# Two transformer blocks on one core: how rotations, score masks, sinks and gates are made, and where four pieces of work stand

## The chip, the cores and the metric

The kernel runs on one core of one Trainium2 chip. The metric is the device time of one execution in microseconds (us); of several runs, the median. PE is TensorE, ACT ScalarE, DVE VectorE, POOL GpSimd, and SP the engine that issues the loads.

## What is computed

Input is x, 512 tokens by 1024 features, float32. `first_block` runs twice (two layers: latent attention with 8 heads and a depthwise convolution of 31 taps beside it, output projection, gated feed-forward part with a short convolution), then `second_block` once. The parts that the change touches, cut from the reference:

```python
def rope(x, pos):                       # second block: queries and keys, heads of 64
    x1, x2 = xf[..., :half], xf[..., half:]
    return concatenate([x1 * cos - x2 * sin, x2 * cos + x1 * sin])
...
ckv = vmap(compress)(stack([k_c, v_c]), cmp_pos, cmp_w1, cmp_w2)     # gelu(blocks @ w1) @ w2, 31 blocks
o_cmp, p_cmp = compressed_attention(qn, ckv[0], ckv[1], t)
o_slc = selected_attention(qn, k_s, v_s, idx, t)
o_win = banded_attention(qn, k_w, v_w, NSA_WINDOW, None)
gates = sigmoid(g_n).reshape(B, S, NSA_KV, NSA_GROUP, NSA_BRANCHES)
o_nsa = gates[..., 0:1] * o_cmp + gates[..., 1:2] * o_slc + gates[..., 2:3] * o_win
o_swa = banded_attention(qw, kw, v_sw, SWA_WINDOW, sinks)            # window 128, a sink per head
    # s masked outside the band; m = max(s, sk); den = sum(exp(s - m)) + exp(sk - m)
```

With 512 tokens every block is selected, so `o_slc` is plain causal attention. In `first_block` the softmax runs over all 512 keys.

## The kernel before

Activations lie transposed, 128 features by 512 tokens per chunk. Every large product is exact to float32 by halves: weights come from memory into `raw` (a ring of four slabs), ACT rounds a slab into `w_hi` (`split`, L1083), DVE subtracts for `w_lo` (L1445), and PE does three matmuls per chunk (`mm3`, L516 to L518). `w_hi` and `w_lo` hold two slabs, so slab n+2 can be split only when PE has finished slab n. Each engine runs its own list of instructions in the order written; semaphores connect them (`wait_ge`, `then_inc`; a helper `Tally` only counts). No scheduler reorders anything: what stands earlier in an engine's list holds up what stands behind it.

**Attention of a layer of `first_block`** (PE L662, L691, L703). Work goes in 16 units, a pair of heads by 128 queries. In step s PE does `scores(s)`, `turn(s - 2)` (transposes of the probabilities) and `values(s - 3)`. DVE's `attend` takes the negative maximum (L1638) and the reciprocal of the sums (L1630), with four convolution taps (L1578) between units; 124 taps in all have to be done by the end. ACT's `attend` does the exponentials (L1227), `normalise` (L1209: scaling by the reciprocal, a pair of heads at a time) and `turned` (L1216: transposes out of PSUM). After units 0 to 2 ACT and DVE each split one slab, S_UKV + 1 + SPL, which is slab S_O + 1, a part of the output projection's weights.

**Projections of `second_block`** (`T_ORDER`, 13 slabs: `vc`, and then 12 chunks that are rotated, `ROPED`: kc, ks, kw, kx, four qn, four qx). PE puts slab i into bank i % 4. ACT copies the bank into `tz` (L1313). The rotation needs the two halves of 32 features of each head exchanged: PE multiplies `tz` by a permutation matrix (`swap_halves`, L776, float32, two passes) into bank 4 or 5, and DVE's `rope` (L1742, L1743, L1752) forms cos times `tz` plus sin times the swapped bank. DVE's loop also does, per i, a split, one of eight scalings of x (L1775, i = 3 to 10) and at i = 2 and 3 `blocks` (L1723 to L1729: the overlapping key and value blocks for `compress`), at i = 4 and 5 `blocks_low` (L1734). Then four slabs of untransposed values and gate columns (`VG`, 408 columns) go into banks 0 to 3, and PE computes `compress` (8 slabs, matmuls of 256 columns). ACT copies the values (L1332, L1333), forms the gates by Sigmoid (L1335) and the Gelu (L1340), and loads the table of log and exp (L1088) before it copies `hid`, `kcT` and `vcn` (L1345 to L1349), on which the small products L844, L849 and then L863 wait. The exponentials of the compressed scores come at L1352.

**Attention of `second_block`**: 48 units in the same three-stage scheme (`scores2`, `turn2`, `values2`). A unit sees n key chunks of 128 (1 to 4; in the sliding-window units, 16 of the 48, one at t = 0 and two otherwise). Its scores go to bank pair `S2_B[u % 2]`; on top PE adds masks as bf16 matmuls (diagonal L892, previous chunk L891) and, in sliding-window units, writes the sink into the column behind the scores (L895, float32, one column), for each head of the pair.

## Time and profile before

| | |
|---|---|
| median of 3 runs | 1944.41 us (1942.99 to 1944.85) |
| the profiled execution's own time | 1946.59 us |
| its span | 1944.8 us |
| PE, DVE, ACT busy | 96%, 68%, 48% of the span |
| mean granted PE clock | 0.985 |
| first layer, second layer, second block, last projection part | roughly 0 to 600, 600 to 1225, 1225 to 1530, 1530 to 1945 us |

All times of views are microseconds from the span's start. A clock of 1.00 is 2.4 GHz, 0.50 is 1.2 GHz. A timeline row gives start, duration, engine, line, operation, tiles, count of merged instructions, and in brackets how long the engine had been idle before and what ended that. A matmul's duration includes its drain; the pace of a stream is the distance of its starts.

### The profile page before, as it was taken

The numbers are of one execution on the slowest core, as the hardware profiler recorded it, in microseconds if no ns is written. First come the engines' busy times: TensorE is split into PE (matmuls) and PEld (weight loads), VectorE is DVE, ScalarE is ACT, GpSimd is POOL, SyncE is SP. The second block draws the span as 40 slices with busy tenths as digits, with TensorE's granted clock in tenths as the row PEclk, the third lists the DMA queues.
The fourth block names the chain that finished last, engine by engine and source line by source line (L and its number), as shares of the span: only waits on it lengthen the run. The fifth ranks groups of instructions, "written<-read, shape, count | busy, mean of one in ns | idle before, by whom it ended". The sixth has DMA issues, their size and how long they took to land.

```text
span 1944.8 us, 27183 instructions
## 1 busy us (share of the span) xinstructions
PE 1875.1 (96%) x9099; PEld 1477.2 (76%) x9099; DVE 1322.9 (68%) x1890; ACT 927.3 (48%) x1473; POOL 176.2 (9%) x130
## 2 busy tenths in 40 slices
PE   6999999999999999999999999998898999999998
PEld 5775688888888775678888888777565778888887
DVE  6899667777655799767777655773767377777544
ACT  5468554444433457664444433324656554444322
POOL 0000220000132000130000033000012300000010
PEclk9999999999999999999999999998899999999999
DMA  5220133333234321023333233334000223333332
GB/s 164 69 78 23 33 97 95 97 94 93 84 99 110 79 79 34 12 87 98 97 97 97 79 97 104 88 82 130 1 1 1 76 65 97 97 97 88 89 96 74
DMA packets 285096, 154.47 MB, mean 79 GB/s; under 512 B 16949, under 2 KB 283095, under 8 KB 285015
## 3 DMA queue, kind: packets, MB, share of 16 engines
q1 hardware_dynamic: 284596, 153.26, 27.4%
q8 instruction: 46, 0.75, 0.2%
q14 instruction: 35, 0.29, 0.0%
q10 hardware_dynamic: 419, 0.17, 0.0%
HBM read 151.31 MB, written 2.10 MB: 79 GB/s over the span
## 4 chain that ended last, share of the span: by engine, by line
PE 83%; DVE 8%; issue 4%; ACT 4%; DMA 0%; DVEq 0%; SPq 0%; ACTq 0%
PE bank L516 24%; PE bank L518 24%; PE bank L517 24%; DVE cacc L1578 2%; PE bank L887 1%; PE bank L929 1%; PE bank L908 1%; DVE w_lo L1445 1%; DVE nmax L1638 1%; PE bank L662 1%; ACT w_hi L1083 1%; PE bank L895 1%; PE bank L530 0%; ACT pr L1209 0%; DMA x_in<-in_x 0%
## 5 line engine op out<-in xcount | busy, mean ns | idle before, releaser
L1083 ACT ACTIVATE w_hi<-raw 128x1024 fp32r<-128x1024 f32 (+3 forms) x345 | 336.9, 984 | 605.2 <-PE bank L518 599.2
L1445 DVE TENSOR_TENSOR w_lo<-raw,w_hi 128x1024 fp32r<-128x1024 f32 (+3 forms) x345 | 407.4, 1188 | 314.6 <-ACT w_hi L1083 313.1
L516 PE MATMUL bank<-h_hi,w_hi 128*128 128x512 f32 x1448 | 575.9, 398 | 5.9 <-DVE w_lo L1445 5.6
L518 PE MATMUL bank<-h_hi,w_lo 128*128 128x512 f32 x1448 | 564.8, 390 | 0.0
L517 PE MATMUL bank<-h_lo,w_hi 128*128 128x512 f32 x1448 | 564.7, 390 | 0.0
L516 PEld LDWEIGHTS bank<-h_hi,w_hi 128*128 128x128 f32 x1448 | 272.5, 188 | 71.6 <-issue 11.3
L517 PEld LDWEIGHTS bank<-h_lo,w_hi 128*128 128x128 f32 x1448 | 272.4, 188 | 61.6 <-issue 6.3
L518 PEld LDWEIGHTS bank<-h_hi,w_lo 128*128 128x128 f32 x1448 | 272.4, 188 | 57.2
L516 PE MATMUL bank<-a_hi,w_hi 128*128 128x512 f32 x528 | 206.1, 390 | 0.0
L518 PE MATMUL bank<-a_hi,w_lo 128*128 128x512 f32 x528 | 205.5, 389 | 0.0
L517 PE MATMUL bank<-a_lo,w_hi 128*128 128x512 f32 x528 | 205.4, 389 | 0.0
L1578 DVE SCALAR_TENSOR_TENSOR cacc<-u_pad,lc,cacc 128x512 f32<-128x512 f32 x240 | 168.1, 751 | 1.6
L1526 DVE TENSOR_TENSOR zr<-bank,rstd 128x512 f32<-128x512 f32 x132 | 90.8, 688 | 83.1 <-PE bank L518 68.8
L1532 DVE SCALAR_TENSOR_TENSOR tz<-zr,lc,tz 128x511 f32<-128x511 f32 x176 | 131.9, 750 | 19.5 <-DVE tz L1532 6.8
L1149 ACT ACTIVATE a_hi<-tz 128x512 f32 (+1 forms) x66 | 41.7, 633 | 160.7 <-DVE tz L1540 160.7
L518 PEld LDWEIGHTS bank<-a_hi,w_lo 128*128 128x128 f32 x528 | 99.1, 188 | 20.7
L517 PEld LDWEIGHTS bank<-a_lo,w_hi 128*128 128x128 f32 x528 | 99.1, 188 | 20.5
L516 PEld LDWEIGHTS bank<-a_hi,w_hi 128*128 128x128 f32 x528 | 99.1, 188 | 20.3
L1542 DVE TENSOR_TENSOR a_lo<-tz,a_hi 128x512 f32 x66 | 45.7, 693 | 61.5 <-ACT a_hi L1149 61.5
L1145 ACT ACTIVATE tz<-zr,lc 128x512 f32<-128x512 f32 x88 | 71.1, 808 | 28.8 <-DVE zr L1526 28.8
L1931 POOL TENSOR_TENSOR sq<-x 128x512 f32 (+1 forms) x14 | 27.4, 1959 | 616.3 <-DVE x L1704 616.3
L1532 DVE SCALAR_TENSOR_TENSOR tz<-zr,cols,tz 128x510 f32<-128x510 f32 x88 | 65.9, 749 | 9.5 <-DVE tz L1532 1.7
(295 smaller groups left out, 2227.7 us busy)
## 6 DMA issues: line engine op xcount, KB each, us to landing
raw<-in_w_up SPq DMA_DIRECT2D x132, 512.0 KB, 3.8
raw<-in_w_in SPq DMA_DIRECT2D x39, 512.0 KB, 3.9
raw<-in_w_down SPq DMA_DIRECT2D x48, 384.0 KB, 3.3
raw<-in_w_down SPq DMA_DIRECT2D x48, 320.0 KB, 3.1
raw<-in_w_o SPq DMA_DIRECT2D x16, 512.0 KB, 3.4
raw<-in_cmp_w SPq DMA_DIRECT2D x8, 512.0 KB, 3.8
raw<-in_w_out SPq DMA_DIRECT2D x8, 512.0 KB, 3.7
raw<-in_w_uq SPq DMA_DIRECT2D x8, 288.0 KB, 2.9
```

The lines of the kernel that those rows point to most:

```text
L516: mm(o, wh, mh, start=start, stop=False)
L517: mm(o, wh, ml, start=False, stop=False)
L518: return mm(o, wl, mh, start=False, stop=stop)
L1083: last = A_(dst(w_hi), src(raw), ACT.Copy)
L1145: A_(tz[:, s, :], zr[:, s % 2, :], ACT.Identity, bias=c_b(ch), scale=c_w1(ch)).then_inc(z1_done.sem, 1)
L1149: A_(a_hi[:, bass.ds(i * 2 + j, 1), :], tz[:, 2 * j + 1:2 * j + 2, :], ACT.Copy).then_inc(ah_done.sem, 1)
L1445: last = v.tensor_tensor(dst(w_lo), src(raw), dst(w_hi).bitcast(f32), ALU.subtract)
L1526: v.tensor_tensor(zr[:, s % 2, :], bank[s][:, :], rstd[:, 0, :], ALU.mult).then_inc(zr_done.sem, 1)
L1532: ins = v.scalar_tensor_tensor(tz[:, s, a:b], zr[:, s % 2, a + sh:b + sh], tap(n, ch), tz[:, s, a:b], ALU.mult, ALU.add)
L1542: v.tensor_tensor(a_lo[:, bass.ds(i * 2 + j, 1), :], tz[:, 2 * j + 1:2 * j + 2, :], a_hi[:, bass.ds(i * 2 + j, 1), :].bitcast(f32), ALU.su ...
L1578: ins = v.scalar_tensor_tensor(cacc[:, c, :], src, wc, cacc[:, c, :], ALU.mult, ALU.add)
L1931: link(p.tensor_tensor(sq[:, :], chunk, chunk, ALU.mult))
```

## The change

1. **Halves swapped by ACT.** PE's `swap_halves` is gone. After the copy into `tz`, ACT copies the same bank four more times, 32 partitions each and into the neighbour's place, into a new tile `swapped`, which DVE's `rope` reads instead of a bank. PE's slab i waits until slab i - 4's swap is made. The values go to banks 4, 5, 1, 2.
2. **Blocks later.** `blocks` moves from i = 2, 3 to i = 6, 9, `blocks_low` with ACT's rounding of `xe` from i = 4, 5 to i = 8, 11, and the scalings of x from i = 3 to 10 to i = 5 to 12.
3. **Gates by exponential.** ACT computes exp(-g) (L1348 of the changed kernel), with the negated scale in a new tile `r_neg`; DVE adds 1 and takes the reciprocal. The load of the table of log and exp moves behind `vcn`.
4. **Sinks once per bank pair.** Only units with t < 2 write the sink, before their scores; units with t = 2 and 3 find it in the bank. A unit with one chunk puts it in columns 128 to 255, so that the sink's column is 256 in all. The two masks of a unit with two chunks become one matmul of 256 columns with `band_b`.
5. **Third pair scaled sooner.** In the first block's attention, ACT does `normalise(2)` and `turned(1)` right behind the exponentials of unit 2, and DVE `inverse(2)`; the split of slab S_O + 1 moves to the end (ACT behind step 17, DVE behind step 18).

```diff
-            def swap_halves(r):
-                pe.wait_ge(rc_done.sem, r + 2)
-                if r >= 2:
-                    pe.wait_ge(rope_done.sem, r - 1)
-                mm(bank[4 + r % 2][:, :], const[:, K_SWAP:K_SWAP + P], tz[:, r % 2, :], start=True, stop=True)\
-                    .then_inc(sw_done.sem, 1)
...
+                if i >= 5:
+                    pe.wait_ge(sw_done.sem, i - 4)
...
-                if i >= 2:
-                    swap_halves(i - 2)
...
-            swap_halves(len(ROPED) - 1)
+            pe.wait_ge(sw_done.sem, len(ROPED) - 2)
...
+                c0 = first_col(b, t)
+                if b == SC_SWA and t < 2:
+                    for e in range(2):
+                        mm(o[e][:, 2 * P:2 * P + 1], ones[0:1, :], sinks[0:1, 2 * c + e:2 * c + e + 1], start=True, stop=True)
...
                     if n == 2 and b == SC_SWA:
-                        mm(o[e][:, 0:P], eye_b[:, :], prev_b[:, :], start=False, stop=False)
-                    last = mm(o[e][:, (n - 1) * P:n * P], eye_b[:, :], diag_b[:, :], start=False, stop=True)
-                    if b == SC_SWA:
-                        last = mm(o[e][:, n * P:n * P + 1], ones[0:1, :], sinks[0:1, 2 * c + e:2 * c + e + 1], start=True, stop=True)
+                        last = mm(o[e][:, 0:2 * P], eye_b[:, :], band_b[:, :], start=False, stop=True)
+                    else:
+                        last = mm(o[e][:, c0 + (n - 1) * P:c0 + n * P], eye_b[:, :], band_b[:, P:2 * P], start=False, stop=True)
...
                 attend(2)
-                split(L, g, S_UKV + 1 + SPL)
+                normalise(2)
+                turned(1)
                 for s in range(3, SU + 4):
                     attend(s)
+                    if s == SU + 1:
+                        split(L, g, S_UKV + 1 + SPL)
...
+                for h in range(4 * (i > 0)):
+                    last = A_(swapped[h * 32:(h + 1) * 32, (i - 1) % 2, :], bank[i % 4][(h ^ 1) * 32:((h ^ 1) + 1) * 32, :], ACT.Copy, scale=sc)
+                if i > 0:
+                    last.then_inc(sw_done.sem, 1)
...
-                A_(gates[:, t * NG:(t + 1) * NG], bank[t][:, 2 * P:2 * P + NG], ACT.Sigmoid,
-                   scale=r_in[:, t:t + 1]).then_inc(gate_done.sem, 1)
+                A_(gates[:, t * NG:(t + 1) * NG], VG_B[t][:, 2 * P:2 * P + NG], ACT.Exp,
+                   scale=r_neg[:, t:t + 1]).then_inc(gate_exp.sem, 1)
...
-                link(v.tensor_tensor(tz[:, 3, :], bank[4 + r % 2][:, :], const[:, K_SIN:K_SIN + SEQ], ALU.mult))
+                link(v.tensor_tensor(tz[:, 3, :], swapped[:, r % 2, :], const[:, K_SIN:K_SIN + SEQ], ALU.mult))
...
-                if 3 <= i < 3 + KD:
-                    c = i - 3
+                if 5 <= i < 5 + KD:
+                    c = i - 5
...
+            dve.wait_ge(gate_exp.sem, NT)
+            link(v.tensor_scalar(gates[:, :], gates[:, :], 1.0, None, ALU.add))
+            v.reciprocal(gates[:, :], gates[:, :]).then_inc(gate_done.sem, 1)
```

Three places in the order of the instructions. First, ACT at the start of the first block's attention, from the copy of unit 0's transposes on (`pr` probabilities, `pt` their transposes, `w_hi` a split slab). Before:

```order
L1209 ACTIVATE pr<-pr,rinv 128x512 x2
L1216 ACTIVATE pt<-bank 128x512 x2
L1226 REGISTER_ALU
L1227 ACTIVATE pr,rsum<-bank,nmax 128x512
L1226 REGISTER_ALU
L1227 ACTIVATE pr,rsum<-bank,nmax 128x512
L1083 ACTIVATE w_hi<-raw 128x1024
L1226 REGISTER_ALU
L1227 ACTIVATE pr,rsum<-bank,nmax 128x512
L1226 REGISTER_ALU
L1227 ACTIVATE pr,rsum<-bank,nmax 128x512
L1206 REGISTER_ALU
```

and now:

```order
L1213 ACTIVATE pr<-pr,rinv 128x512 x2
L1220 ACTIVATE pt<-bank 128x512 x2
L1230 REGISTER_ALU
L1231 ACTIVATE pr,rsum<-bank,nmax 128x512
L1230 REGISTER_ALU
L1231 ACTIVATE pr,rsum<-bank,nmax 128x512
L1210 REGISTER_ALU
L1213 ACTIVATE pr<-pr,rinv 128x512 x2
L1220 ACTIVATE pt<-bank 128x512 x2
L1230 REGISTER_ALU
L1231 ACTIVATE pr,rsum<-bank,nmax 128x512
```

The scaling of unit 2 and the copy of unit 1's transposes now stand ahead of the exponentials of unit 3, and no split stands there.

Second, ACT from the gates to the compressed scores. Before:

```order
L1335 ACT_TABLE_LOAD
L1335 ACTIVATE gates<-bank,r_in 128x24 x4
L1083 ACTIVATE w_hi<-raw 128x1024 x4
L1340 ACT_TABLE_LOAD
L1340 ACTIVATE hidc<-bank 62x256
L1083 ACTIVATE w_hi<-raw 128x1024 x4
L1340 ACTIVATE hidc<-bank 62x256
L1088 ACT_TABLE_LOAD
L1345 ACTIVATE hid<-bank 128x62 x4
L1347 ACTIVATE kcT<-bank 128x62
L1349 ACTIVATE vcn<-bank 31x128
L1352 ACTIVATE cs<-cs 128x496 x2
```

and now:

```order
L1348 ACTIVATE gates<-bank,r_neg 128x24 x4
L1087 ACTIVATE w_hi<-raw 128x1024 x4
L1353 ACT_TABLE_LOAD
L1353 ACTIVATE hidc<-bank 62x256
L1087 ACTIVATE w_hi<-raw 128x1024 x4
L1353 ACTIVATE hidc<-bank 62x256
L1357 ACTIVATE hid<-bank 128x62 x4
L1359 ACTIVATE kcT<-bank 128x62
L1361 ACTIVATE vcn<-bank 31x128
L1092 ACT_TABLE_LOAD
L1365 ACTIVATE cs<-cs 128x496 x2
```

Of three table loads two are left, and the last stands behind `vcn`.

Third, PE in one sliding-window unit with t = 2 (L887 scores, L908 transposes, L929 values). Before:

```order
L887 MATMUL bank<-k_kx,qx 128x256 x2
L891 MATMUL bank<-prev_b,eye_b 128x128
L892 MATMUL bank<-diag_b,eye_b 128x128
L895 MATMUL bank<-sinks,ones 128x1
L891 MATMUL bank<-prev_b,eye_b 128x128
L892 MATMUL bank<-diag_b,eye_b 128x128
L895 MATMUL bank<-sinks,ones 128x1
L908 MATMUL bank<-const,pr_86 128x128 x2
```

and now, two such units and the beginning of the one that follows, which has t = 0:

```order
L893 MATMUL bank<-k_kx,qx 128x256 x2
L897 MATMUL bank<-band_b,eye_b 128x256 x2
L912 MATMUL bank<-const,pr_87 128x128 x2
L933 MATMUL bank<-pt_88,v_78 64x128 x4
L893 MATMUL bank<-k_kx,qx 128x256 x2
L897 MATMUL bank<-band_b,eye_b 128x256 x2
L912 MATMUL bank<-const,pr_87 128x128 x4
L933 MATMUL bank<-pt_88,v_78 64x128 x2
L891 MATMUL bank<-sinks,ones 128x1 x2
L893 MATMUL bank<-k_kx,qx 128x128 x2
L899 MATMUL bank<-band_b,eye_b 128x128 x2
```

Behind the scores stand two matmuls where six stood; the sinks are written only ahead of the scores of t = 0 and 1.

## Rows read from the trace of the kernel before

**Rows 1.** The page, part 1 (busy us, share) and PE's waits over the span (total, times, longest).

```profile
PE 1875.1 (96%) x9099; PEld 1477.2 (76%) x9099; DVE 1322.9 (68%) x1890; ACT 927.3 (48%) x1473; POOL 176.2 (9%) x130
...
PE bank L691 <- ACT pt L1216: 13.2, 10, 3.7
```

**Rows 2.** Timeline of PE, projections of the second block.

```profile
1234.21 0.39 PE L516 MATMUL bank<-h_hi,w_hi 128*128 128x512 f32 x1
...
1239.65 1.02 PE L776 MATMUL bank<-tz,const 128*128 128x512 f32 x2
...
1246.00 1.02 PE L776 MATMUL bank<-tz,const 128*128 128x512 f32 x2
...
1307.41 1.12 PE L776 MATMUL bank<-tz,const 128*128 128x512 f32 x2 [0.85 <-ACT tz L1313]
1307.97 0.75 PE L516 MATMUL bank<-w_hi,h_hi 128*128 128x408 f32 x1
```

**Rows 3.** Timeline of ACT: a split and a copy there, two copies of 64 partitions earlier.

```profile
1293.10 1.06 ACT L1083 ACTIVATE w_hi<-raw 128x1024 fp32r<-128x1024 f32 x1 [4.80 <-PE bank L518]
...
133.54 1.22 ACT L1201 ACTIVATE kT<-bank 64x512 f32<-64x512 f32 x2 [0.51 <-PE bank L518]
```

**Rows 4.** Timeline of DVE in the projections' loop: `blocks`, iteration 5, and a query's last step.

```profile
1254.95 2.69 DVE L1723 COPY xe<-vc_raw 64x248 f32<-64x248 f32 x8
...
1259.00 1.22 DVE L1445 TENSOR_TENSOR w_lo<-raw,w_hi 128x1024 fp32r<-128x1024 f32 x1
...
1262.12 2.79 DVE L1752 TENSOR_TENSOR k_kw<-tz 64x512 f32<-64x512 f32 x4
...
1276.43 0.69 DVE L1752 TENSOR_TENSOR qn<-tz 128x512 f32<-128x512 f32 x1
```

**Rows 5.** Timelines of ACT and PE from the gates to the compressed scores.

```profile
1330.14 1.28 ACT L1335 ACT_TABLE_LOAD   x1
...
1334.48 0.39 PE L516 MATMUL bank<-w_hi,xe_hi 128*128 128x256 f32 x1 [3.84 <-DVE w_lo L1445]
...
1348.82 1.28 ACT L1088 ACT_TABLE_LOAD   x1
...
1350.60 1.08 PE L844 MATMUL bank<-hid,w2k 128*128 128x62 f32 x4 [1.41 <-ACT hid L1345]
...
1353.02 7.04 PE L863 MATMUL bank<-kcT,qn 64*128 64x31 f32 x64 [0.36 <-ACT vcn L1349]
...
1363.44 1.20 ACT L1352 ACTIVATE cs<-cs 128x496 f32<-128x496 f32 x2 [10.47 <-DVE cs L1802]
```

**Rows 6.** Timeline of PE: masks and sinks of a sliding-window unit with two chunks.

```profile
1427.51 0.23 PE L891 MATMUL bank<-prev_b,eye_b 128*128 128x128 bf16 x1
1427.57 0.22 PE L892 MATMUL bank<-diag_b,eye_b 128*128 128x128 bf16 x1
1427.72 0.38 PE L895 MATMUL bank<-sinks,ones 1*128 1x1 f32 x2
...
1428.56 0.44 PE L908 MATMUL bank<-const,pr 128*128 128x128 f32 x2
```

**Rows 7.** First layer's attention: timelines of DVE and PE.

```profile
151.01 1.23 DVE L1445 TENSOR_TENSOR w_lo<-raw,w_hi 128x1024 fp32r<-128x1024 f32 x1 [1.45 <-ACT w_hi L1083]
152.15 1.28 DVE L1638 TENSOR_REDUCE nmax<-bank 128x1 f32<-128x512 f32 x2
...
161.86 0.69 DVE L1638 TENSOR_REDUCE nmax<-bank 128x1 f32<-128x512 f32 x1 [1.90 <-PE bank L662]
...
156.08 1.97 PE L691 MATMUL bank<-const,pr 128*128 128x128 f32 x8 [3.74 <-ACT pt L1216]
```

**Rows 8.** Stretches: us, busy PE, PEld, DVE, ACT, POOL, granted clock, DMA.

```profile
156.00:160.00 4.00, 3.92 (x25) 3.26 (x25) 3.93 (x8) 3.74 (x10) 0.00 (x0) 0.50 0.23 78
...
1421.48:1432.15 10.67, 10.67 (x90) 7.32 (x88) 6.35 (x22) 5.70 (x22) 1.58 (x2) 1.00 0.00 0
1353.00:1357.00 4.00, 3.98 (x38) 3.98 (x38) 0.00 (x0) 0.00 (x0) 0.00 (x0) 0.50 0.07 24
```

More of the change, by code:

```diff
@@ L107, in keys_of, with first_col @@
     return (max(0, t - 1), min(2, t + 1)) if b == SC_SWA else (0, t + 1)
+def first_col(b, t):
+    return P if b == SC_SWA and t == 0 else 0
 HALVES = [0]
@@ L174, in build @@
         lneb = sb("lneb", [P, 1])
+        r_neg = sb("r_neg", [P, NT])
         lc = sb("lc", [P, LCOLS])
@@ L238, in build @@
         v2 = at("v2", [P, NT, 3 * P], 32 * KB)
+        swapped = at("swapped", [P, 2, SEQ], 68 * KB)
         ct_all = at("ct_all", [P, PAIRS, NT, 2, P], 38 * KB)
@@ L260, in build @@
         STAT = bank[7]
+        VG_B = bank[4], bank[5], bank[1], bank[2]
         C_B, CT_B = (bank[4], bank[5]), (bank[6], bank[7])
@@ L809, in _ @@
                         k = i * VG_K + kk
-                        last = mm3(bank[t][:, 0:VG], (h_hi[:, k, tok], h_lo[:, k, tok]),
+                        last = mm3(VG_B[t][:, 0:VG], (h_hi[:, k, tok], h_lo[:, k, tok]),
                                    (w[0][:, kk, :], w[1][:, kk, :]), k == 0, k == KD - 1)
@@ L1311, in _ @@
                     act.wait_ge(rope_done.sem, i - 2)
+                sc = HD2 ** -0.5 if kind[0] == "q" else 1.0
                 dst = vc_raw[:, :] if kind == "vc" else tz[:, (i - 1) % 2, :]
-                A_(dst, bank[i % 4][:, :], ACT.Copy, scale=HD2 ** -0.5 if kind[0] == "q" else 1.0).then_inc(rc_done.sem, 1)
+                A_(dst, bank[i % 4][:, :], ACT.Copy, scale=sc).then_inc(rc_done.sem, 1)
+                for h in range(4 * (i > 0)):
+                    last = A_(swapped[h * 32:(h + 1) * 32, (i - 1) % 2, :], bank[i % 4][(h ^ 1) * 32:((h ^ 1) + 1) * 32, :], ACT.Copy, scale=sc)
+                if i > 0:
+                    last.then_inc(sw_done.sem, 1)
                 if i == 0:
@@ L1322, in _ @@
                     A_(r_in[:, :], bank[6][:, 0:NT], ACT.Copy).then_inc(rcol_done.sem, 1)
-                if i in (4, 5):
-                    t = i - 4
+                    A_(r_neg[:, :], bank[6][:, 0:NT], ACT.Copy, scale=-1.0).then_inc(rcol_done.sem, 1)
+                if i in (8, 11):
+                    t = i // 11
                     act.wait_ge(xe_f.sem, t + 1)
@@ L1328, in _ @@
                 step2(S2_V + i)
-            act.wait_ge(rcol_done.sem, 1)
+            act.wait_ge(rcol_done.sem, 2)
             for t in range(NT):
                 r = r_in[:, t:t + 1]
-                A_(v2[:, t, 0:2 * P], bank[t][:, 0:2 * P], ACT.Copy, scale=r).then_inc(v2_done.sem, 1)
-                A_(v2[:, t, 2 * P:3 * P], bank[t][:, 2 * P + NG:VG], ACT.Copy, scale=r).then_inc(v2_done.sem, 1)
+                A_(v2[:, t, 0:2 * P], VG_B[t][:, 0:2 * P], ACT.Copy, scale=r).then_inc(v2_done.sem, 1)
+                A_(v2[:, t, 2 * P:3 * P], VG_B[t][:, 2 * P + NG:VG], ACT.Copy, scale=r).then_inc(v2_done.sem, 1)
             for t in range(NT):
-                A_(gates[:, t * NG:(t + 1) * NG], bank[t][:, 2 * P:2 * P + NG], ACT.Sigmoid,
-                   scale=r_in[:, t:t + 1]).then_inc(gate_done.sem, 1)
+                A_(gates[:, t * NG:(t + 1) * NG], VG_B[t][:, 2 * P:2 * P + NG], ACT.Exp,
+                   scale=r_neg[:, t:t + 1]).then_inc(gate_exp.sem, 1)
             for t in range(2):
@@ L1362, in _ @@
                         st = 2 * (s % 4) + e
-                        A_(pr2[:, s % 3, e, 0:n], S2_B[s % 2][e][:, 0:n], ACT.Exp, bias=nmax[:, st:st + 1],
+                        c0 = first_col(b, t)
+                        A_(pr2[:, s % 3, e, 0:n], S2_B[s % 2][e][:, c0:c0 + n], ACT.Exp, bias=nmax[:, st:st + 1],
                            accum_out=rsum[:, st:st + 1]).then_inc(e_done.sem, 1)
@@ L1654, in _ @@
                 conv(3)
-                split(g, S_UKV + 1 + SPL)
+                inverse(2)
                 for s in range(3, SU + 5):
                     attend(s)
+                    if s == SU + 2:
+                        split(g, S_UKV + 1 + SPL)
                     conv(4)
@@ L1778, in _ @@
                     rope(i - 2)
-                if i == 2:
+                if i == 6:
                     blocks(0)
-                if i == 3:
+                if i == 9:
                     blocks(1)
-                if i in (4, 5):
-                    blocks_low(i - 4)
+                if i in (8, 11):
+                    blocks_low(i // 11)
             rope(len(ROPED) - 1)
```

25 lines of the change are left out of this document (12 added, 13 removed).

## The prediction, made before the changed kernel ran

> **What bounds the kernel now.** I read the page's part 1 first, then PE's waits, then the stretches, then the timelines of the four places that the change touches. PE is busy 96% of the span [rows 1], so outside a few places only matmul time that goes away shortens anything, and inside them a wait of PE does. Of what PE waits for, the largest is L691, transposes in the first block's attention: 13.2 us in 10 waits, at most 3.7 at a time [rows 1]. Behind such a wait the granted clock can stand at 0.50 [rows 8], so a wait costs more than its length. I take as unit of account the profiled execution (1946.59 us, span 1944.8); the median of the runs is 2.2 us lower, and I subtract the same gain from it. About 0.2%, 3.9 us, is what a measurement of this kernel can tell from no change.
>
> **Rotations.** A slab of projections takes PE 5.44 us (slab 2: 1234.21 to 1239.65), and with a swap the distance to the next swap is 6.35 [rows 2]: a swap costs 0.91 us, and there are 12, so 10.9. The last swap waits 0.85 for the last copy [rows 2], which goes too, since the values no longer need the last bank. That is 11.8 us of PE, plus some small waits for `w_lo` now.
>
> What takes their place is on ACT and DVE, which must fit into 5.44 us instead of 6.35. ACT: a split takes 1.06 and ACT is then idle for 4.80 before the next [rows 3]. A copy of 32 partitions by 512 from a bank is not in the trace; nearest is the copy of 64 partitions, two in 1.22, 0.61 each [rows 3]. Step i becomes 0.96 for the split, 0.6 for the copy, 4 x 0.61: 4.0 us, below 5.44. Bounds: a copy's time goes by its 512 columns, so I see no reason for less than 0.48 (its duration less an overlap) nor, since the split of 1024 columns takes 1.06, for more than that. DVE: iteration 5, with a key, runs from 1259.00 to 1264.91, 5.9 us (split, scaling of x, two products, four additions), a query's one addition takes 0.69 instead of 2.79 [rows 4], so 3.8; `blocks` takes 1254.95 to 1259.00, 4.05 [rows 4], `blocks_low` 1.2 by its size. The split for slab i+2 is ready in time if DVE has finished iteration i-1 some 4.2 us after the end of slab i. I carried this on slab by slab (slab end, ACT's split 0.26 later, DVE's split behind it or behind its last iteration). For the kernel before it gives the values' end 0.2 us from the traced one. For the changed kernel DVE lags 7 us behind a slab's end through the keys (iterations 3 to 5), 9 to 10 after iterations 6 and 9, which carry `blocks`, and PE waits 0.5 at slab 12 and 0.7 at the third slab of values, behind DVE's last rotations. So 12 less small waits: **12.0 us** (10.5 if each copy costs 1.0; 12.3 at 0.49). The scalings of x end two iterations later, and SP waits for them before it loads `compress`'s weights: that load would start near 1301.5 instead of 1301.9 and is wanted near 1309.7, covered. `r_neg` is one tiny copy more on ACT, in its idle time.
>
> **Gates and table loads.** ACT loads the Sigmoid's table for 1.28 us between the copies of the values and the third split of `compress`, for whose result PE waits 3.84 [rows 5]. Exp is in the table that is loaded anyway, so the wait becomes 2.56: 1.28 less. The second load, 1348.82 to 1350.10, stands ahead of `hid`; L844 waits 1.41 for that [rows 5]. Moved behind `vcn` it falls into ACT's 10.47 us of idle time before L1352 [rows 5]; L844 can start when the second L830 has ended, 1.2 us sooner. DVE's addition and reciprocal of 128x96 fall before the end of L863, where DVE waits for 10 us, and cost nothing; were that cover gone, 0.5. Sum **2.5 us**, at least 1.3 if one of the two is hidden by a split that is late anyway.
> The trace has the load at 1.28 us. The Trainium skill (ScalarE: Activation LUTs, What ACT_TABLE_LOAD costs) prices a switch at about 2.7 us with its drain; by that the two would be worth 5.3. The row decides.
>
> **Sinks and masks.** Behind the scores of a unit with two chunks come 1.05 us (1427.51 to 1428.56) of masks and sinks [rows 6]. A mask of 128 columns sets the pace at 0.06 (1427.51 to 1427.57), so two of 256 columns take 0.13 each at most, 0.25. With t = 2 and 3, 8 units, that is all: 0.8 less each, 6.4 us. With t = 0 and 1, also 8 units, the sinks stay: the two passes of one head go 0.38 [rows 6] with their drain, 0.31 by the start of what follows, so 0.6 for both heads. That leaves 0.2 less each, 1.6 to 1.8. Together **8.2 us** if PE stays the bound there. A unit then takes PE 1.8 to 2.1 us instead of 2.6; in a stretch of four units, 10.67 us, DVE is busy 6.35 and ACT 5.70 [rows 8], 1.6 and 1.4 us a unit, so there is just room. Bounds: 4 (DVE's evictions come through as waits), 9.
>
> **Third pair.** ACT's split stands behind the exponentials of unit 2, and DVE, after 1.45 of idle time, does its part from 151.01, so that the maximum of unit 3 starts at 152.15 and its exponentials behind that; unit 2 is scaled only behind them, and PE waits 3.74 for its transposes' turn [rows 7]; then the clock is at 0.50 from 156 to 160 [rows 8], scores come late and DVE idles 1.90 [rows 7]. With the new order the sums of unit 2 are there at 150.0 (where the split began), its scaling ends at 151.5, the copies of unit 1 at 152.4, about when PE has finished the scores of unit 4 (152.2): no wait of note. DVE's maximum of unit 3 starts at 150.15, 2.0 sooner, and unit 4's 2.0 sooner as well; behind it DVE sets the pace (3.9 us a unit: 1.28 for the maxima [rows 7], the rest taps) and the idle 2.07 does not come back: 4.1 us. PE meets one wait of 1.3 us at unit 3, whose scaling now stands behind the exponentials of unit 4; DVE's pace hides it. What is late next: at the end DVE must still do the split (1.2), between its last tap, some 5 us before PE wants the sums of the convolution, and those sums; it is covered, since slab S_O + 1 is wanted only after them. The loads that wait for this slab (S_O + 4, S_O + 5) start near 210 and are wanted near 228. So 4.1 per layer, **8.2 us** for two; at least 1.0 each (DVE's own idle time of 1.45 [rows 7], less 0.45 that it will wait for the sums), at most 5.
>
> **Sum.** 12.0 + 2.5 + 8.2 + 8.2 = 30.9: 1946.6 becomes 1915.7, the median 1944.4 becomes **1913.5 us**.
>
> **Rivals.**
> *A. The clock stays up in `compress`.* L863's 64 matmuls take 7.04 us [rows 5] at a granted 0.50 [rows 8], after waits of 3.84, 1.23 and 1.41. With the first at 2.56 and the third near 0.2 the clock might not fall: L863 would take 3.5 and the products before it 0.6 less, 4 us more gained: 1909.5. Against it: 2.3 us of `w_lo` waits stay in between, and the 1.23. 15%. What the page says goes the same way (the Trainium skill, TensorE: Matmul & The Clock Gate, HAM oscillation: idle gaps of PE throttle it, and the transition is paid again each time).
> *B. Part of the gain turns into new waits.* In the sliding-window units DVE or ACT becomes the bound (gain 4 instead of 8.2), or the first block's attention gives only the 1.0 per layer that DVE's idle time holds (2 instead of 8.2). For it: DVE works at its limit from 163 us on. 1918 to 1920. 17%.
> *C. Slower: the swap overloads ACT.* ACT becomes the pace of the projections when four copies and the rest pass 5.44, that is when a copy of 32 partitions costs over 0.97 us. To eat the gains elsewhere (18.9) and be 0.2% slower it must cost some 1.8: step 8.8, 12 steps, 40 us more than 5.44 each, less 11.8: 1944.4 - 18.9 + 28.5 = 1954. Nothing in the rows has 512 columns on ACT above 0.72. 2%.
> *D. It comes out level*, by B and C in part: 1%.
>
> **Numbers.** The forecast has 65% and its own range is 1910.5 to 1917. The range to hold 8 in 10 reaches into A and B: 1909 to 1920. Faster 0.97, same 0.01, slower 0.02.
>
> **What would show it.** No matmul of the swap between slabs, distances of 5.44 between slabs, `swapped` copies near 0.6 and the first matmul of the values some 12 us nearer to the projections' start; a wait near 2.6 in place of 3.84 and none for `hid`; no table load at the gates; 2.0 us between the starts of sliding-window units with t = 2 and 3; L691's waits down by 3.7 in each layer with the clock at 1.00 around 156 us, and the layer's end 4 us earlier. I am wrong if copies of 32 partitions take over 1 us, if PE waits over 2 us in all for `w_lo` in the projections, if DVE's maxima rather than PE set the pace of the sliding-window units, or if the 4 us of an attention come back as a wait before L735.

## The result, and the profile after

| | before | changed |
|---|---|---|
| median (range, runs) | 1944.19 us (1942.99 to 1944.85, 4) | 1922.26 us (1919.63 to 1924.50, 4) |
| profiled execution: own time, span | 1946.59, 1944.8 | 1924.50, 1922.4 |

The ratio is 0.989, 95% interval 0.9877 to 0.9902. The change gains 21.9 us where 30.9 were forecast; 1922.3 lies above the range of 1909 to 1920. Of all executions reported in this document one, of e1 below, took 2125.76 us at a mean granted clock of 0.841 against 0.979 to 0.995 elsewhere, and is left out of its ratio. The page of the changed kernel, part 1, and PE's waits over the span (total, times, longest):

```profile
PE 1856.1 (97%) x9019; PEld 1465.5 (76%) x9019; DVE 1322.8 (69%) x1892; ACT 955.2 (50%) x1521; POOL 176.0 (9%) x130
...
PE bank L700 <- ACT pt L1220: 9.2, 10, 1.7
PE bank L912 <- DVE pr L1886: 7.7, 7, 2.2
```

Against [rows 1] PE is busy 19.0 us less; its waits for the first block's transposes (L700 now) fell from 13.2 to 9.2, and a group has grown, the transposes of the second block that wait for DVE's scaling (L912), 7.7 us where the kernel before has 4.8.

Where the time went is read from seven markers on PE's timeline, each the start of the first or last row of merged matmuls with a given pair of operands: the first scores of a layer's attention and the sum over its convolution; the first matmul of `compress`; the first scores of the second block's attention (ks); the first and last of the sliding-window scores (kx); the last kw scores. The differences, in us:

| stage | before | changed | gain | forecast |
|---|---|---|---|---|
| first layer's attention | 82.58 | 79.55 | 3.0 | 4.1 |
| second layer's attention | 82.65 | 79.54 | 3.1 | 4.1 |
| sum of layer 2 to `compress` (projections, values) | 511.50 | 500.17 | 11.3 | 12.0 |
| `compress` to first ks scores | 33.58 | 29.35 | 4.2 | 2.5 |
| first ks to first kx scores | 48.24 | 48.26 | 0 | 0 |
| first to last kx scores | 42.75 | 40.53 | 2.2 | 8.2 |
| last kx to last kw scores | 44.73 | 47.89 | -3.2 | 0 |

One profile of each kernel stands behind this table, and a stage that two kernels share can differ between their profiles by where the clock fell: over the kernels below that leave a stage as it was, an attention takes 81.39 to 82.65 us, `compress` 32.25 to 33.58 and the kx stage 42.75 to 44.22.

**Projections.** ACT's timeline over one slab, and PE's row where the first values begin:

```profile
1233.47 1.06 ACT L1087 ACTIVATE w_hi<-raw 128x1024 fp32r<-128x1024 f32 x1
1234.55 0.60 ACT L1321 ACTIVATE tz<-bank 128x512 f32<-128x512 f32 x1
1235.18 2.39 ACT L1323 ACTIVATE swapped<-bank 32x512 f32<-32x512 f32 x4
1238.91 1.06 ACT L1087 ACTIVATE w_hi<-raw 128x1024 fp32r<-128x1024 f32 x1 [1.34 <-PE bank L527]
...
1289.63 0.34 PE L525 MATMUL bank<-w_hi,h_hi 128*128 128x408 f32 x1
```

Two splits are 5.44 us apart, as forecast; a copy of 32 partitions takes 0.60 (2.39 for four), and ACT still has 1.34 of idle time. The first values stand at 1289.63 instead of 1307.97 [rows 2]: 18.3 us sooner, of which 6.6 had been gained by the end of layer 2's attention, so 11.8 here, as forecast. PE's waits for `w_lo` in this stage are 0.51 (1284.04) and 0.59 (1299.33), against 0.5 and 0.7 in the forecast.

**Compress.** Timelines of PE and ACT:

```profile
1315.30 0.48 PE L525 MATMUL bank<-w_hi,xe_hi 128*128 128x256 f32 x1 [2.55 <-DVE w_lo L1459]
...
1331.65 6.29 PE L865 MATMUL bank<-kcT,qn 64*128 64x31 f32 x64 [0.36 <-ACT vcn L1361]
1331.62 1.28 ACT L1092 ACT_TABLE_LOAD   x1
1341.24 1.20 ACT L1365 ACTIVATE cs<-cs 128x496 f32<-128x496 f32 x2 [8.35 <-DVE cs L1818]
```

Against [rows 5]: the wait of 3.84 is 2.55, the one for `hid` is gone (0.36 for `vcn` is left ahead of L865), and the last table load lies inside ACT's idle time.

**Sliding-window units.** DVE, POOL and PE around the first eviction of `yw` (DVE's copy of a finished bank into the tile `yw`), then stretches (us, busy PE, PEld, DVE, ACT, POOL, granted clock, DMA):

```profile
1403.74 0.68 DVE L1849 COPY yw<-bank 128x512 f32<-128x512 f32 x1
1404.34 0.75 DVE L1870 TENSOR_REDUCE nmax<-bank 128x1 f32<-128x257 f32 x2
1404.50 1.04 POOL L1950 TENSOR_TENSOR sq<-yw 128x512 f32<-128x512 f32 x1 [181.79 <-DVE yw L1849]
1405.19 1.84 DVE L1886 TENSOR_SCALAR pr<-pr,rinv 128x256 f32<-128x256 f32 x2
1405.62 1.27 POOL L1951 TENSOR_TENSOR ssq<-ssq,sq 128x512 f32<-128x512 f32 x1
1407.09 0.67 PE L912 MATMUL bank<-const,pr 128*128 128x128 f32 x4 [0.94 <-DVE pr L1886]
...
1406.00:1410.00 4.00, 3.06 (x20) 2.39 (x20) 2.12 (x6) 1.65 (x6) 0.88 (x1) 0.70 0.00 0
1410.00:1414.00 4.00, 4.00 (x22) 2.41 (x20) 1.31 (x5) 1.51 (x5) 0.00 (x0) 0.50 0.00 0
```

The two scalings of 128x256, 0.62 us elsewhere in this stretch, take 1.84 while POOL squares and adds: they end at 1407.03, 0.14 behind the end of POOL's addition (1406.89). With the eviction and the maximum in front of them DVE needs 0.68 + 0.75 + 0.16 + 1.84 = 3.4 us for this unit; four units take PE 8.24 now (1396.67 to 1404.91), and the scores of t = 3 start 1.8 us behind those of t = 2 (1401.38, 1403.15; 2.0 forecast). So PE waits 0.94 (and again, 0.94 and 1.47, at the next two evictions), and the granted clock goes to 0.50 behind the wait. In the kernel before the clock was 1.00 there and PE had no such wait, although the same operation was slowed there as well. Its DVE and POOL, and the stretch of four units that follows the one of [rows 8]:

```profile
1423.34 0.62 DVE L1867 TENSOR_SCALAR pr<-pr,rinv 128x256 f32<-128x256 f32 x2
1431.84 1.46 DVE L1867 TENSOR_SCALAR pr<-pr,rinv 128x256 f32<-128x256 f32 x2
1431.61 1.27 POOL L1932 TENSOR_TENSOR ssq<-ssq,sq 128x512 f32<-128x512 f32 x1
...
1432.15:1442.82 10.67, 10.67 (x90) 7.32 (x88) 7.10 (x22) 5.64 (x22) 2.31 (x3) 1.00 0.01 2
```

The stretch of [rows 8], on which the forecast rests, ends 0.31 us into the slowed scaling, with DVE busy 6.35 us; this one has 7.10.

**First block's attention.** PE and DVE behind unit 3, then the stretches:

```profile
157.32 1.15 PE L700 MATMUL bank<-const,pr 128*128 128x128 f32 x8 [1.73 <-ACT pt L1220]
158.40 1.98 PE L712 MATMUL bank<-pt,vN 128*64 128x128 f32 x16
160.31 2.68 PE L671 MATMUL bank<-kT,qT 96*128 96x512 f32 x4
...
162.17 0.69 DVE L1652 TENSOR_REDUCE nmax<-bank 128x1 f32<-128x512 f32 x1 [0.95 <-PE bank L671]
...
156.00:160.00 4.00, 2.68 (x24) 2.41 (x24) 4.00 (x9) 3.81 (x10) 0.00 (x0) 0.79 0.00 0
160.00:164.00 4.00, 4.00 (x20) 2.18 (x18) 2.88 (x6) 2.61 (x6) 0.00 (x0) 0.78 0.00 0
```

The wait of 3.74 [rows 7] is gone and one of 1.73 has come at unit 3 (1.3 forecast); but the clock falls behind this one too, scores come late, and DVE idles 1.12 (0.95 and 0.17) of the 2.07 that it idled there before (1.90 in [rows 7] and 0.17).

### The profile page after: what moved, and what is told of

The parts are those of the page before. It is cut to its first block, busy times and chain, and to the rows that moved or that the text cites. A ratio compares the mean times of both kernels' runs of the same rounds, so it can differ in the third digit from the quotient of the medians.

```text
span 1922.4 us, 27065 instructions
## 1 busy us (share of the span) xinstructions
PE 1856.1 (97%) x9019; PEld 1465.5 (76%) x9019; DVE 1322.8 (69%) x1892; ACT 955.2 (50%) x1521; POOL 176.0 (9%) x130
## 4 chain that ended last, share of the span: by engine, by line
PE 82%; DVE 10%; ACT 4%; issue 4%; DMA 0%; DVEq 0%; SPq 0%; ACTq 0%
PE bank L525 24%; PE bank L527 24%; PE bank L526 24%; DVE cacc L1592 2%; PE bank L893 1%; PE bank L933 1%; DVE w_lo L1459 1%; PE bank L912 1%; DVE nmax L1652 1%; DVE pr L1886 1%; DVE nmax L1870 1%; PE bank L671 1%; PE bank L539 0%; ACT pr L1213 0%; DMA x_in<-in_x 0%
## 5 line engine op out<-in xcount | busy, mean ns | idle before, releaser
L525 PEld LDWEIGHTS bank<-h_hi,w_hi 128*128 128x128 f32 x1448 | 272.6, 188 | 68.3 <-issue 8.7
```

What stands on the lines that cost most here:

```text
L525: mm(o, wh, mh, start=start, stop=False)
```

## The experiments

Stage times of the profiled executions, by the same markers (att. 1 and 2: the two attentions; kx: first to last kx scores; kw: last kx to last kw scores):

| kernel | median us | att. 1 | att. 2 | compress | kx | kw |
|---|---|---|---|---|---|---|
| before | 1943.5 | 82.58 | 82.65 | 33.58 | 42.75 | 44.73 |
| e1 sinks, masks | 1941.23 | 81.39 | 81.61 | 32.63 | 38.97 | 46.37 |
| e2 third pair | 1938.43 | 78.25 | 79.59 | 32.40 | 42.76 | 46.13 |
| e3 rotations | 1933.95 | 81.47 | 81.63 | 33.37 | 44.22 | 44.73 |
| e4 gates, tables | 1942.28 | 82.21 | 82.46 | 27.50 | 44.22 | 46.01 |
| e5 changed, again | 1921.40 | 79.55 | 79.46 | 29.51 | 38.98 | 46.12 |
| e6 no squares | 1913.45 | 79.57 | 79.48 | 29.55 | 33.63 | 42.30 |
| e7 held back in vain | 1921.17 | 78.24 | 79.57 | 29.26 | 40.50 | 47.89 |
| e8 filler, kx | 1917.44 | 79.60 | 79.54 | 29.21 | 35.93 | 46.38 |
| e9 squares later | 1913.45 | 79.46 | 78.27 | 29.06 | 33.63 | 45.43 |
| e10 filler, attention | 1920.85 | 78.26 | 79.19 | 28.53 | 40.49 | 46.06 |
| e11 filler, compress | 1920.73 | 79.63 | 79.58 | 26.02 | 38.83 | 46.41 |
| e12 taps moved | 1923.07 | 79.59 | 79.59 | 29.15 | 38.86 | 46.43 |
| e13 before, later | 1943.44 | 82.37 | 82.53 | 32.39 | 42.76 | 45.92 |
| e14 e1 and later | 1930.61 | 82.32 | 82.58 | 32.25 | 33.62 | 42.58 |
| e15 e9 and fillers | 1909.61 | 79.21 | 79.24 | 25.64 | 33.62 | 45.44 |

The median of before is that of the runs beside e1 to e4; it is 1943.6 beside the others. The groups e1 to e4, e5 to e8, e9 to e12 and e13 to e15 ran on one chip each, the kernel before beside them. A ratio goes by all executions of a kernel and of its partner, so it need not be the quotient of the two medians (for e4 that is 0.9994, the ratio 1.0003).

### The four parts alone

Each is the kernel before with one part of the diff.

**e1**, part 4 (sinks and masks):

> The kernel before, with the sinks once per bank pair and the joined masks alone. My theory: PE's work per sliding-window unit shrinks as forecast (2.0 us between units with t = 2 and 3), but DVE's eviction of yw and its scaling beside POOL's squares then come out as waits of 0.9 to 1.5 us at the transposes, and the granted clock falls behind each; so that from the first kx scores to w_out's start hardly 1 us is left and the whole kernel gains 0 to 3 us (ratio 0.9985 to 1.000). Rival 1: the units are not to blame, the loss comes from how the other parts of the change shift the block in time; then this alone gains 7 to 8.5 us (ratio 0.996). Rival 2: slower by the fallen clock, 1 to 3 us.

Measured 1941.23 us, ratio 0.999 (0.9981 to 1.0): some 2.2 us of the 8.2, at the edge of what the runs can tell. PE's waits in 1404 to 1450 us, and a stretch behind one of them:

```profile
PE bank L916 <- DVE pr L1876: 3.3, 3, 1.4
...
1436.00:1440.00 4.00, 4.00 (x22) 2.61 (x18) 0.94 (x4) 0.79 (x3) 0.00 (x0) 0.50 0.00 0
```

The three waits and the low clock come with this part alone: my theory, and rival 1 falls.

**e2**, part 5 (third pair):

> The kernel before, with the third pair scaled sooner alone. My theory: DVE is busy without a gap from 164 us to 203 us of the first layer in either kernel, so that only the idle time of DVE that vanishes is gained: 3.0 us per layer, 6.1 in all (ratio 0.9969); the wait of PE at the transposes of unit 3 is 1.7 us and the granted clock still falls to half behind it. Rival: the forecast's 4.1 per layer, 8.2 in all (ratio 0.9958), the rest being eaten in the changed kernel by something else.

Measured 1938.43 us, ratio 0.9975 (0.9965 to 0.9984): 5.1 us. The interval holds my theory's 0.9969 and not the rival's 0.9958. But the two layers of the profile differ. PE in the first, and the stretches:

```profile
156.45 1.15 PE L691 MATMUL bank<-const,pr 128*128 128x128 f32 x8 [1.72 <-ACT pt L1216]
157.52 1.09 PE L703 MATMUL bank<-pt,vN 128*64 128x128 f32 x16
...
156.00:160.00 4.00, 3.55 (x28) 2.37 (x28) 4.00 (x8) 3.82 (x9) 0.00 (x0) 1.00 0.00 0
160.00:164.00 4.00, 4.00 (x30) 2.41 (x28) 4.00 (x8) 3.73 (x9) 0.00 (x0) 1.00 0.00 0
```

The same wait of 1.72, but here the clock stays at 1.00, DVE does not idle behind it, and the layer takes 78.25: 4.3 us less than before, as much as the forecast's 4.1. In its second layer the time is 79.59, as in the changed kernel. Whether the clock falls behind this wait differs from one pass to the next, and is worth 1.3 us.

**e3**, part 1 and 2 (rotations, blocks):

> The kernel before, with the halves swapped by ACT, the blocks later and the values' banks alone. My theory: 11.3 us, as between the markers of the two kernels (projections to the first compress matmul), so ratio 0.994; compress keeps the Sigmoid's table load, the wait of 3.8 us and its low clock. Rival: part of compress's extra gain (4.2 us measured, 2.5 forecast) comes from here, by w_lo being ready sooner; then 12.5 to 13 us. DVE's last rotations as the pace of the values would show as 10 or less.

Measured 1933.95 us, ratio 0.9954 (0.994 to 0.9969): 9.5 us. From the sum of layer 2 to `compress` it takes 500.07 us, 11.4 less than before. Compress keeps its 33.37: the rival falls. In the kx stage, which this part leaves as it was, 1.5 us are lost (44.22 for 42.75): the clock was 0.64 in 1409 to 1413 us, though PE has no wait between 1393 and 1439.

**e4**, part 3 (gates, table load):

> The kernel before, with the gates by exponential and the moved table load alone. My theory: two loads of 1.28 us go from PE's path, 2.5 us, and because the wait of PE for w_lo is 2.6 instead of 3.8 and none stands ahead of the small products, the clock stays at 1.00 some microseconds longer: 4.2 us in all (ratio 0.9978). Rival: 2.5 us only (0.9987), the clock then falling as before. Rival 2: under 1 us, another wait takes the place of the loads.

Measured 1942.28 us, ratio 1.0003 (0.999 to 1.0016). The profiled execution gained 6.1 us in compress, more than either theory, since no clock fell there until L865, which took 6.00. But the whole was not measurably faster: the twelve executions run from 1937.63 us (mean granted clock 0.989) to 1950.84 (0.979), while 28 of before stay within 1941.66 and 1945.90. What this part saves is smaller than what the clock moves. Why this kernel spreads more is open.

By their medians the four gain 2.2, 5.1, 9.5 and 1.2 us, 18.0 together, and the whole change 21.9; with intervals of 1.8 to 2.8 us to either side of each, this difference settles nothing.

### The sliding-window units

**e5**, the changed kernel again:

> The changed kernel as it is, on the chip of the three runs that follow, so that they have a partner: 1920 to 1924 us, ratio 0.989. In its own row of times the span should fall with the mean granted clock: the parts run alone gave 1935.8 us at 0.989 and 1949.0 us at 0.979 for one and the same kernel.

1921.40 us, ratio 0.9883 (0.9868 to 0.9899); spans of 1917.0 at a mean clock of 0.988 to 1921.3 at 0.984.

**e6**, POOL's share of the work taken away for the first three of the four chunks (the kernel leaves out three quarters of the sum of squares of this branch):

```diff
-            squares(N, 1, PAIRS, lambda c: yw[:, c, :], lambda c: pool.wait_ge(y_done.sem, y_done.at(N, 2 + c + 1)), 1)
...
+                    link(p.tensor_tensor(sq[:, 0:1], yw[:, c, 0:1], yw[:, c, 0:1], ALU.mult))
+                    p.tensor_tensor(ssq[:, 0:1], ssq[:, 0:1], sq[:, 0:1], ALU.add).then_inc(ssq_done.sem, 1)
```

> The changed kernel with POOL's squares and additions for the first three chunks of yw made on one column (so the sum of squares of that branch leaves out three quarters of its terms). My theory: DVE's scaling of 128x256 twice takes 0.62 us everywhere instead of 1.84, PE's three waits of 0.9 to 1.5 us at the transposes of t = 2 go, the clock stays at 1.00 for most of 1386 to 1440, and 3.4 us of waits plus 2 to 4 us of slow matmuls are gained: 1914 to 1917 us. Rival: the eviction of yw (0.68) alone is enough for waits of 0.7 and more, little changes (within 1 us of the changed kernel).

1913.45 us, ratio 0.9845 (0.9832 to 0.9859): 8.0 us better than e5, and PE has no wait of note left in the kx stage although the eviction is still there, so the rival falls. DVE's groups in 1384 to 1428 us, of e6 and then of e5:

```profile
L1886 DVE TENSOR_SCALAR pr<-pr,rinv 128x256 f32<-128x256 f32 x24 | 7.4, 350 | 0.4
```

```profile
L1886 DVE TENSOR_SCALAR pr<-pr,rinv 128x256 f32<-128x256 f32 x22 | 10.4, 516 | 0.4
```

The same scaling at a mean of 350 ns, and of 516 with POOL beside some of them. The rule in the Trainium skill (SBUF — State Buffer, SBUF: two separate sides) goes the same way: DVE and GpSimd share a pair of ports under an exclusive lock, held for a whole instruction. The trace agrees: the slowed scalings of the changed kernel end 0.14 us behind the end of POOL's addition. The maxima, which read PSUM, stay at 0.75 beside POOL.

**e7** and **e9** hold the squares back with all work done. In e7 the semaphore that POOL waited for had long been counted up:

```diff
+                if c < PAIRS - 1:
-                    pool.wait_ge(r_done.sem, r_done.at(N, 2 * (UNITS.index((SC_SWA, c + 1, 0)) + 1)))
+                    pool.wait_ge(r_done.sem, r_done.at(N, 2 * (UNITS.index((SC_SWA, c + 1, NT - 1)) + 1)))
```

(the line with the minus is e7's, the other e9's).

> The changed kernel with POOL's squares of the first three chunks of yw held back until DVE has scaled the first unit of the next chunk, so that they fall on units whose scaling has 128x128 and slack. All work is done. My theory: same total work on each engine, but the peak of eviction, maximum and slowed scaling in one step is spread over two; PE's waits at the transposes of t = 2 shrink from 0.9 to 1.5 us to under 0.5, and 3 to 6 us are gained: 1915 to 1919 us. Rival: the slowing only moves to another unit and PE waits there as long: within 1 us of the changed kernel.

e7: 1921.17 us, ratio 0.9883; POOL's first square stood at 1402.59 behind an eviction at 1401.82, so it tests nothing and only repeats e5.

> In the run before, the semaphore that should have held POOL back had long been counted up: the squares started 0.09 us behind the eviction as ever. Now POOL waits until DVE has scaled the last unit of the chunk that is being evicted into, two steps later, so that the squares start some 3 to 4 us after the eviction and fall on a unit whose scaling has 128x128. All work is done. My theory: PE's waits at the transposes of t = 2 (0.9 to 1.5 us, three times) shrink to 0 to 0.5, and 3 to 6 us are gained on the changed kernel: 1915 to 1919 us, the clock at 1.00 for most of 1386 to 1425. Rival: the slowing of 1.2 us moves to another unit and makes PE wait there as long: 1920 to 1922 us.

e9: 1913.45 us, ratio 0.9846 (0.9833 to 0.986), as good as taking the work away. Timelines of POOL and DVE, then PE's waits and a stretch:

```profile
1405.89 1.04 POOL L1950 TENSOR_TENSOR sq<-yw 128x512 f32<-128x512 f32 x1 [184.64 <-DVE pr L1886]
1407.01 1.27 POOL L1951 TENSOR_TENSOR ssq<-ssq,sq 128x512 f32<-128x512 f32 x1
...
1402.14 0.69 DVE L1849 COPY yw<-bank 128x512 f32<-128x512 f32 x1
1403.60 0.61 DVE L1886 TENSOR_SCALAR pr<-pr,rinv 128x256 f32<-128x256 f32 x2
1407.87 0.69 DVE L1886 TENSOR_SCALAR pr<-pr,rinv 128x128 f32<-128x128 f32 x2
1423.20 1.15 DVE L1883 TENSOR_TENSOR rinv<-rinv,gates 128x2 f32<-128x2 f32 x1
...
PE bank L912 <- DVE pr L1886: 1.0, 3, 0.4
...
1404.00:1408.00 4.00, 4.00 (x40) 2.87 (x40) 2.35 (x10) 2.54 (x11) 2.04 (x2) 1.00 0.01 2
```

POOL's 2.3 us now fall where DVE waits for scores (it idled 1.25 ahead of 1407.00) and reads PSUM; the scaling that they still meet takes 0.69 instead of 0.48, in the first and second chunk. Behind the third they meet a product of 128x2, which takes 1.15 instead of 0.16: even the smallest operation is held up for as long as POOL's runs (1423.06 to 1424.33). My theory had the peak spread over two units; what happened is better than that, most of the slowing is gone.

**e8**, PE kept busy in the wait:

```diff
+                if b == SC_SWA and t == 2 and c >= 1:
+                    pe.wait_ge(pt_done.sem, pt_done.at(N, HALVES[u] - 1))
+                    for _ in range(14):
+                        mm(bank[4 + HALVES[u] % 2][:, 0:P], eye_b[:, :], band_b[:, P:2 * P], start=True, stop=True)
```

> The changed kernel with 14 matmuls of 128 columns (bf16, 0.8 us) whose result is overwritten, put in front of PE's wait for the scaling of unit t = 2 of chunks 1 to 3, so that PE is busy while it waits. My theory: DVE still ends as late, so the transposes start no sooner, but the granted clock no longer falls behind these waits, and the 2 to 4 us of slow matmuls are gained: 1917 to 1920 us. Rival: the clock falls in this stretch as often as before whatever PE does in the 0.9 us, since it also fell in a kernel that had no wait there (rotations alone, 0.64 at 1409 to 1413 us): within 1 us of the changed kernel, or slower by the fillers (up to 0.5).

1917.44 us, ratio 0.9863 (0.9848 to 0.9878): 4.0 us better than e5. DVE's scaling is as late as ever; e8's stretch and, below it, e5's:

```profile
1416.00:1420.00 4.00, 3.84 (x40) 2.80 (x39) 2.38 (x9) 1.55 (x6) 0.36 (x1) 1.00 0.00 0
```

```profile
1416.00:1420.00 4.00, 3.50 (x20) 2.47 (x20) 1.53 (x6) 1.29 (x5) 0.29 (x1) 0.65 0.00 0
```

So of the 8.0 us, by the medians, some 4 are the waits and some 4 the clock behind them. The kx stage of the profiles gives shares of the same order: 33.62 us without waits (e9), 35.93 with two waits filled and the clock at 1.00 (e8), 38.98 (e5) to 40.53 (the changed kernel's profile above) with the clock falling: 2.3 us for the waits, 3.1 to 4.6 for the clock.

**e13** and **e14**, e9's delay put into the kernel before, and into e1:

> Control: the kernel before, with nothing changed but that POOL holds the squares of yw back as in the run above. In the kernel before PE hid the slowed scaling behind its longer units (its waits there were 0.5 us, and 1.1 to 2.2 later). My theory: nothing to gain, 0 to 1 us (ratio 0.9995 to 1.0). Rival: the slowing beside POOL cost the kernel before as much as the changed one, then 4 us or more (ratio under 0.998).

> The kernel before with the sinks once per bank pair and the joined masks (which alone gained 2.2 us) and the squares of yw held back. My theory: now the forecast's 8.2 us for this part come, and 1 to 2 more since the clock falls less often: 8 to 11 us (ratio 0.9943 to 0.996). Rival: 2 to 4 us, if the 8 us of the run above need the shorter rotations or another part of the change.

e13: 1943.44 us, ratio 0.9997 (0.9988 to 1.0006), nothing. e14: 1930.61 us, ratio 0.9936 (0.9922 to 0.9949), 13.0 us, more than I expected. In the kernel before, the slowed scaling was hidden by PE's longer units; the shorter units uncovered it. The kx stage takes 42.76 us in e13 and 33.62 in e14, 9.1 less (8.2 forecast); most of the rest comes from the clock, which stayed at 1.00 afterwards in e14's profile (kw 42.58) and fell in e13's (kw 45.92), behind the same wait of 2.19.

### Attention and compress

**e10** puts 28 matmuls like those of e8 into bank 3 ahead of `turn(3)`'s wait (the transposes of unit 3) in both layers, **e11** 17, 42, 17, 16 and 19 of them ahead of the waits of `compress`.

> The changed kernel with 28 matmuls of 128 columns (bf16, 1.6 us) into a bank that is not in use, in front of PE's wait of 1.7 us for unit 3's transposes in both layers. Measured so far from the first scores to the sum over the convolution: 82.6 us in the kernel before, 79.55 in the changed one where the clock fell to 0.79 behind the wait, 78.2 in two kernels where it did not fall. My theory: with PE busy it never falls, 78.2 us in both layers, so 1 to 2.6 us are gained on the changed kernel: 1919 to 1920.5 us. Rival: the fall has another cause, or the gain behind it is taken back by DVE's taps: 79.5 us and 1921 to 1922 us.

e10: 1920.85 us, ratio 0.9884 (0.9869 to 0.9899). The clock no longer fell behind unit 3 in either layer, and the first took 78.26. In the second it fell behind a later wait of 1.74 at the layer's end that I had not filled (0.58 in 796 to 800 us), and it took 79.19. The whole, between my theory and the rival, differs from e5 by less than the measurement tells.

> The changed kernel with matmuls of 128 columns (bf16, 17, 42, 17, 16 and 19 of them, 6.2 us) into a free bank, in front of PE's waits in compress (1.06, 2.57, 1.06, 1.01 for w_lo, 1.23 for hidc). My theory (rival A of the prediction): the waits are why the clock falls; with PE busy it stays at 1.00 in 1312 to 1320 (1.4 us gained) and through L865's 64 small products, which take 3.6 us instead of 6.6 (3 us gained): 1917 to 1918 us. Rival: the small products themselves (31 columns, 0.054 us each) let the clock fall some microseconds after their start, whatever came before: only 1.4 us gained, L865 stays near 6.5, 1920 to 1921 us. If a filler is longer than its wait, up to 0.5 us is lost.

e11: 1920.73 us, ratio 0.9885 (0.987 to 0.99). The small products of e11, and of e15, which has the same fillers:

```profile
1330.60 4.47 PE L869 MATMUL bank<-kcT,qn 64*128 64x31 f32 x64 [0.36 <-ACT vcn L1365]
```

```profile
1329.68 4.06 PE L872 MATMUL bank<-kcT,qn 64*128 64x31 f32 x64 [0.36 <-ACT vcn L1368]
...
1332.00:1336.00 4.00, 3.71 (x38) 2.81 (x36) 2.20 (x4) 0.00 (x0) 0.00 (x0) 0.62 0.19 63
1336.00:1340.00 4.00, 0.00 (x0) 0.00 (x0) 3.86 (x11) 1.90 (x6) 0.00 (x0) 0.50 0.00 0
```

4.5 and 4.1 instead of 6.3, with the clock at 1.00 through all of compress until it fell in the middle of the small products, where PE's last wait was 0.36: the waits bring it down sooner, but they are not the only cause. Compress gained 3.5 us on e5 in the profiled execution; in the median 0.7 are left, within the measurement.

**e12**:

```diff
-                    conv(4)
+                    conv(6 if s == 5 else 4)
```

> The changed kernel with six convolution taps instead of four behind unit 5 of the attention (two fewer at its end), where DVE was idle for 1.1 us in the changed kernel's first layer. My theory: DVE's work sets the end of the attention, so idle time filled with taps is gained where there is idle time: 0 to 1.1 us a layer, the higher where the clock has fallen behind PE's wait: 1919.5 to 1921.5 us. Rival: the later maximum of unit 6 delays PE, which then sets the pace: slower by 0.5 to 1.4 us a layer.

1923.07 us, ratio 0.9901 (0.9886 to 0.9916). DVE's idle time is filled (busy 4.00 in 160 to 164 us), but both layers take 79.59, as in the changed kernel (79.46 to 79.55, clock fallen in all of them). So in these layers nothing is gained and, against the rival, nothing lost either: the transposes that PE waits 1.74 for stand 68.4 us behind the first scores, in e5 68.2 to 68.3. DVE is through 1.4 us sooner at the end (idle 5.19 us there instead of 3.77), which gains nothing. The median is 1.7 above e5's, less than the measurement tells. It is not DVE's sum of work that sets the end of the attention; that it is the time of its last maxima is my reading, which no run here tests.

### The combination

**e15** is the changed kernel with e9's delay and the fillers of e10 and e11.

> The changed kernel with the squares of yw held back, and the fillers in PE's waits of both attentions and of compress. The first alone gave 1913.45, the second about 0.6 and the third about 0.7 us on 1921.4. My theory: they add, since they lie in different places: 1911 to 1912.5 us and a mean granted clock of 0.990 or more. Rival: the clock falls somewhere else instead, as behind the wait of 1.7 us at the end of the second layer's attention: 1913 to 1914 us.

1909.61 us (1904.92 to 1911.03, five runs), ratio 0.9819 (0.9806 to 0.9833): 34 us faster than before and 11.8 faster than e5, with mean clocks of 0.989 to 0.995. Of the 34 us, e9 has 30.1 without fillers. It is more than I expected, but not because the gains add. In the profile the clock fell behind the unfilled wait of 1.74 at the end of both attentions (0.65 in 202 to 206 us), as the rival has it, and the two layers take 158.45 us together, e9's 157.73: there the fillers gained nothing. `compress` is 3.4 us shorter. What else made up 3.8 us in the median is not settled.

## Why the prediction was wrong, step by step

**Rotations, 12.0: right.** 11.3 to 11.4 in every kernel that has them. The copy cost 0.60, ACT fitted into 5.44. The sum was written down 0.6 too high: 11.8 of PE less the new waits of 0.5 and 0.7 is not 12.0. With the waits for `w_lo` of the kernel before that went away (0.21 and 0.56) it comes to 11.4.

**Gates and table loads, 2.5: direction right, size not settled.** The first wait fell by 1.29 and the one for `hid` went, as worked out. The stage gained 4.2 us in the profiled pair (29.1 to 29.6 in most kernels that have the part, 32.3 to 33.6 without). Those two are worth 2.7. Half of the other 1.5 is the small products, 6.29 instead of 7.04 by the clock. That is a small part of rival A; the clock did fall with them (0.51 in 1332.4 to 1336.4 us). e4 could not show the part in the whole.

**Sinks and masks, 8.2: this step failed.** PE's matmul time was right, if a little small: the kx stage loses 9.1 us where nothing else comes through (e13 to e14). Wrong was the check of the cover, "in a stretch of four units, 10.67 us, DVE is busy 6.35 and ACT 5.70 [rows 8], 1.6 and 1.4 us a unit, so there is just room". Units are not alike, and a mean hides the one that has an eviction and a scaling slowed by POOL, 3.4 us. The stretch chosen even ends 0.31 us into that scaling; the next four units have 7.10. The rows were to be had: 0.62 for the scaling in one unit, 1.46 in the one with POOL beside it. What the runs showed in place of "just room": the slowed scaling comes out as waits of PE of 0.94, 0.94 and 1.47, and the clock falls behind them. In the kx stage that is 2.3 us of waits and 3.1 to 4.6 of clock (e8, e5, the profile after), so that 2.2 to 3.8 of the 9.1 came through; the third wait is paid in the stage behind. The lower bound, "4 (DVE's evictions come through as waits)", and rival B named this mechanism, but priced neither the slowed scaling nor the clock. The range, whose top was B's, so ended 2.3 us too low.

**Third pair, 4.1 per layer: mis-sized by the clock.** The chain went as worked out; the wait at unit 3 was 1.73 for 1.3. "DVE's pace hides it" gave it no price. L691's waits were to fall by 3.7 us in each layer; they fell from 13.2 to 9.2 in both together. Without a filler there are 18 passes through this wait, two in each of nine profiles. In 15 of them the clock fell behind it, a layer took 79.46 to 79.63, and the gain on the profile before is 3.0 to 3.2 (against 81.4, which e1 and e3 took with the old order, 1.8). In three (the first layers of e2 and e7, the second of e9) it did not, and the layer took 78.24 to 78.27: 4.3 or 4.4.

**Stages that I did not touch.** I took them as fixed. From the last kx to the last kw scores it took 42.3 to 47.9 us. Two things move it. The third new wait, of 1.1 to 1.5 us, stands there (1430.47 in the profile after, 3.9 us behind the last kx scores), in the kernels with the shorter units and the squares at their old place. And the clock falls or not: behind the wait of 2.19 that every kernel has there it fell in that of before (44.73) and not in e6 or e14 (42.30, 42.58). So part of the -3.2 belongs to the failed step.

Sum for the profiled pair: 3.0 + 3.1 + 11.3 + 4.2 + 2.2 - 3.2 = 20.6, the rest of 22.4 in the start and the end.
